# Layer 1's recurrence gates put two to a PSUM bank and one tile later, the state space layer's sums of squares taken later, the attentions' on TensorE

## The reference, cut to what matters

```
# layer 1: gated linear recurrence and mLSTM
u = rmsnorm(x) @ w_in;  x_l, x_m, z = split(u)
r = sigmoid(einsum(conv(x_l), w_a) + b_a)      # 16 blocks of 128x128
i = sigmoid(einsum(conv(x_l), w_x) + b_x)
a = exp(-8 r softplus(-lam))
h = scan(a, sqrt(1 - a^2) * (i * conv(x_l)))   # the recurrence
... mLSTM heads on x_m, each ended by an rmsnorm over its 512 channels
x = x + (concat(h, y_m) * silu(z)) @ w_out
# layer 2: state space layer, 8 groups
y = (ssd_scan(...) + d_skip * xs) * silu(z)
y = rmsnorm per group of 512 channels;  x = x + y @ w_out
# block 3: S5 branch, 4 gated-linear-attention heads, 4 differential-attention heads
o = rmsnorm over 256 channels of each head, then @ w_br
x = x + (g0*y_a + g1*y_b + g2*y_c) @ w_out;  then a gated MLP and a last rmsnorm
```

## Time and profile before

| | us |
|---|---|
| median of 3 runs | 3475.65 (3473.97 to 3477.48) |
| the profiled execution's own time | 3474.76 |
| its span in the trace | 3472.6 |
| PE busy | 3231.7 (93%) |
| DVE busy | 2320.0 (67%) |
| ACT busy | 1833.2 (53%) |
| POOL busy | 687.3 (20%) |

### The profile page before, as it was taken

One profiled execution on the slowest core, in us unless ns is written; L12 is line 12 of the kernel. 1 busy time (PEld: TensorE's weight loads), 2 busy tenths in 40 slices (PEclk: granted clock), 3 DMA queues, 4 the chain that ended last, 5 costly groups with the idle time before them and its releaser, 6 DMA issues.

```text
span 3472.6 us, 54222 instructions
## 1 busy us (share of the span) xinstructions
PE 3231.7 (93%) x21710; PEld 2944.0 (85%) x21710; DVE 2320.0 (67%) x3235; ACT 1833.2 (53%) x2370; POOL 687.3 (20%) x1118
## 2 busy tenths in 40 slices
PE   6999878999999899998998988998999999999998
PEld 6889878888888888887877877888999888888887
DVE  7655767656666776667666766666656788888544
ACT  5544667544665555654555444333444566666443
POOL 2000000010000000012676775776000100000000
PEclk9999988999999999999999999988999999999999
DMA  5435333555444445555433333333555555555554
GB/s 189 141 134 180 126 109 132 191 188 195 163 156 156 151 152 174 173 188 199 158 105 115 129 121 121 132 131 128 199 184 183 188 192 189 189 191 191 188 188 140
DMA packets 158046, 560.54 MB, mean 161 GB/s; under 512 B 17552, under 2 KB 25808, under 8 KB 157152
## 3 DMA queue, kind: packets, MB, share of 16 engines
q1 hardware_dynamic: 157792, 557.06, 47.6%
HBM read 550.64 MB, written 6.36 MB: 160 GB/s over the span
## 4 chain that ended last, share of the span: by engine, by line
PE 68%; DVE 12%; POOL 10%; ACT 6%; issue 3%; DMA 1%; DVEq 0%; ACTq 0%; POOLq 0%; SPq 0%
PE ps L555 68%; POOL TB L1906 5%; DVE WL L1309 3%; POOL PT L1906 2%; ACT WH L890 2%; POOL BX L1906 2%; ACT L880 1%; POOL BS L1906 1%; POOL SQ L1906 1%; DVE XV L1283 1%; DVE XC L1283 1%; DVE BS L1299 0%; DVE X L1283 0%; DMA RAW<-in_w 0%; ACT SQ L880 0%
## 5 line engine op out<-in xcount | busy, mean ns | idle before, releaser
L555 PE MATMUL ps<-XN,WH 128*128 128x256 f32 (+1 forms) x8864 | 1901.3, 308 | 54.2 <-DVE XN L1272 20.0
L890 ACT ACTIVATE WH<-RAW 128x1024 fp32r<-128x1024 f32 x1010 | 1065.1, 1058 | 1309.2 <-PE ps L555 1276.8
L1309 DVE TENSOR_TENSOR WL<-RAW,WH 128x1024 fp32r<-128x1024 f32 x1010 | 1260.9, 1253 | 518.7 <-ACT WH L890 512.4
L555 PEld LDWEIGHTS ps<-XN,WH 128*128 128x128 f32 x8864 | 1468.2, 197 | 144.8 <-issue 22.2
L555 PE MATMUL ps<-XN,WL 128*128 128x256 f32 x5120 | 1461.8, 285 | 0.0
L555 PEld LDWEIGHTS ps<-XN,WL 128*128 128x128 f32 x5120 | 999.8, 195 | 0.0
L555 PE MATMUL ps<-YS,WH 128*128 128x512 f32 (+1 forms) x1088 | 377.7, 392 | 31.6 <-DVE ZB L1272 29.4
L1906 POOL TENSOR_TENSOR RSB<-RSB,SQ 128x256 f32<-128x256 f32 x75 | 87.5, 1166 | 1244.1 <-ACT SQ L880 1243.1
L555 PE MATMUL ps<-YS,WL 128*128 128x256 f32 x1056 | 296.5, 281 | 0.0
L555 PEld LDWEIGHTS ps<-YS,WH 128*128 128x128 f32 x1088 | 203.9, 190 | 81.9 <-DVE ZB L1272 32.3
L1906 POOL TENSOR_TENSOR SQ<-SQ 128x256 f32<-128x256 f32 (+1 forms) x32 | 37.8, 1182 | 1129.5 <-ACT SQ L880 1127.5
(11 more groups left out here) (327 smaller groups left out, 3423.3 us busy)
## 6 DMA issues: line engine op xcount, KB each, us to landing
RAW<-in_w SPq DMA_DIRECT2D x1010, 512.0 KB, 3.3
CSB<-sums SPq DMA_DIRECT2D x64, 128.0 KB, 3.7
scratch<-X SPq DMA_DIRECT2D x2, 2048.0 KB, 7.8
X<-scratch SPq DMA_DIRECT2D x2, 2048.0 KB, 7.7
X<-in_x SPq DMA_DIRECT2D x4, 512.0 KB, 7.9
X<-in_x SPq DMA_DIRECT2D x1, 2048.0 KB, 7.9
out<-X SPq DMA_DIRECT2D x4, 512.0 KB, 2.6
WIF<-in_w_if SPq DMA_DIRECT2D x1, 576.0 KB, 14.3
```

The lines of the kernel that those rows point to most:

```text
L555: return pe.e.matmul(dst, l, r, start=start, stop=stop, skip_group_check=True)
L890: act.e.activation(WH[:, w % NH, :], RAW[:, w % NB, :], ACT.Copy).then_inc(*act.one(("wh", w)))
L1309: dve.e.tensor_tensor(WL[:, w % NB, :], RAW[:, w % NB, :], WH[:, w % NH, :].bitcast(F32), SUB).then_inc(*dve.one(("wl", w)))
```

## The change

Three edits. In layer 1 the gates of pair q are multiplied after the first `xl` tile of pair q+1, not right behind pair q's own `zl` tiles; the two `ra` blocks share one bank (columns 0 to 255 and 256 to 511), the two `ix` blocks another, and ACT reads both halves once the second block is done. The forced ends of `xl` and `zl` in each pair are gone. In layer 2 the chain has 20 steps: POOL adds at step 13, PE multiplies at 15, ACT takes the root at 16, DVE scales at 17, ACT copies at 18, DVE ends at 19; its forced end stands after the second `zs` tile of the next group. In the attentions POOL no longer adds: PE multiplies both halves by ones into one sum.

```
-    "tail": 6, ... "ssd": 16, ...
+    "tail": 6, ... "ssd": 20, ...
...
-    for q in range(8):
-        for i in range(2):
-            p.append(whole(tile("xl", (2 * q + i,), "e_w_in", 128 * (2 * q + i)), 16))
-        for i in range(2):
-            p.append(whole(tile("zl", (2 * q + i,), "e_w_in", 4096 + 128 * (2 * q + i)), 16))
-        p += [End("xl", (2 * q + 1,)), End("zl", (2 * q + 1,))]
+    for q in range(9):
+        if q < 8:
+            p.append(whole(tile("xl", (2 * q,), "e_w_in", 128 * (2 * q)), 16))
         if q:
-            p.append(End("tail", (q - 1,)))
-        for kind, w in (("ra", "e_lru_wa"), ("ix", "e_lru_wx")):
+            for kind, w in (("ra", "e_lru_wa"), ("ix", "e_lru_wx")):
+                for i in range(2 * q - 2, 2 * q):
+                    p.append(whole(tile(kind, (i,), w, (i, 0), "lru"), 1))
+            p.append(Go("tail", (q - 1,)))
+        if q < 8:
+            p.append(whole(tile("xl", (2 * q + 1,), "e_w_in", 128 * (2 * q + 1)), 16))
             for i in range(2):
-                p.append(whole(tile(kind, (2 * q + i,), w, (2 * q + i, 0), "lru"), 1))
-        p.append(Go("tail", (q,)))
+                p.append(whole(tile("zl", (2 * q + i,), "e_w_in", 4096 + 128 * (2 * q + i)), 16))
+            if q:
+                p.append(End("tail", (q - 1,)))
...
-        if g:
-            p.append(End("ssd", (g - 1,)))
-        else:
+        if g == 0:
             p.append(End("dts", ()))
...
             if j == 0:
                 p.append(Go("ssd", (g,)))
+            if j == 1 and g:
+                p.append(End("ssd", (g - 1,)))
...
-                if start:
+                if start and t.x == "lru" and t.args[0] % 2:
+                    open_[id_] = open_[t.kind, t.args[0] - 1]
+                elif start:
...
-                    dst = banks[0][:, 0:256]
+                    c = 256 * (t.args[0] % 2) if t.x == "lru" else 0
+                    dst = banks[0][:, c:c + 256]
...
-                    pe.wait_ge(*at("gsq", h))
-                    mm(b[:, 0:256], ones, SQ[:, 0, 0:256]).then_inc(*pe.one(("gn", h)))
+                    pe.wait_ge(*at("gsqr", h))
+                    mm(b[:, 0:256], ones, SQ[:, 0, 0:256], True, False)
+                    mm(b[:, 0:256], ones, SQ[:, 0, 256:512], False, True).then_inc(*pe.one(("gn", h)))
```

More of the change, by code:

```diff
@@ L740, in ssd @@
                        True).then_inc(*pe.one(("ymm", g, e_)))
-                if s == 11:
+                if s == 12:
                     kept.discard(holder_of("yb", g, 0))
                     kept.discard(holder_of("yb", g, 1))
-                if s == 13:
+                if s == 15:
                     b = take("side", "y2s", g)
@@ L859, in diff @@
                     b = take("side", "dnm", h)
-                    pe.wait_ge(*at("dsq", h))
-                    mm(b[:, 0:256], ones, SQ[:, 0, 0:256]).then_inc(*pe.one(("dnm", h)))
+                    pe.wait_ge(*at("dsqr", h))
+                    mm(b[:, 0:256], ones, SQ[:, 0, 0:256], True, False)
+                    mm(b[:, 0:256], ones, SQ[:, 0, 256:512], False, True).then_inc(*pe.one(("dnm", h)))
             def last():
@@ L995, in ra @@
             def ra(j, s):
[L996 to L999, removed]
-            def ix(j, s):
-                act.wait_ge(*at("tile", "ix", j))
-                fn(IB[:, j % 2, :], bank("ix", j)[:, 0:256], ACT.Sigmoid, ("ixd", j), ("free", "ix", j),
-                   bias=cv("lru_bx", j))
+                if j % 2:
+                    act.wait_ge(*at("tile", "ra", j))
+                    if j > 1:
+                        act.wait_ge(*at("lruscan", j // 2 - 1))
+                    for i in range(2):
+                        fn(RB[:, i, :], bank("ra", j - 1)[:, 256 * i:256 * i + 256], ACT.Sigmoid, ("free", "ra", j - 1),
+                           bias=cv("lru_ba", j - 1 + i))
+            def ix(j, s):
+                if j % 2:
+                    act.wait_ge(*at("tile", "ix", j))
+                    for i in range(2):
+                        fn(IB[:, i, :], bank("ix", j - 1)[:, 256 * i:256 * i + 256], ACT.Sigmoid, ("ixd", j),
+                           ("free", "ix", j - 1), bias=cv("lru_bx", j - 1 + i))
             def tail(p, s):
@@ L1086, in ssd @@
                         fn(SQ[:, w, :], flat(YB[:, 2 * w:2 * w + 2, :]), ACT.Square, ("ysqr", g))
-                if s == 13:
+                if s == 16:
                     act.wait_ge(*at("y2s", g))
                     rsqrt(RS3, bank("y2s", g)[:, 0:256], 512, ("rsy", g), ("free", "y2s", g))
-                if s == 14:
+                if s == 18:
                     act.wait_ge(*at("yn", g))
@@ L1587, in ssd @@
                     tt(YB, YB, ZB, MUL, ("yz", g))
-                if s == 14:
+                if s == 17:
                     dve.wait_ge(*at("rsy", g))
@@ L1591, in ssd @@
                         stt(YB[:, j, :], YB[:, j, :], cv("gnorm", 4 * g + j), RS3, MUL, MUL, ("yn", g))
-                if s == 15:
+                if s == 19:
                     dve.wait_ge(*at("y2h", g))
@@ L1934, in ssd @@
             def ssd(g, s):
-                if s == 12:
+                if s == 13:
                     pool.wait_ge(*at("ysqr", g))
                     halves(("ysq", g))
[L1939 to L1947, removed]
             def phases(b, r):
@@ L1992, in gpsimd @@
                 "wo": lambda n, s: squares(3, n), "dn": lambda n, s: squares(4, n), "heads": heads, "ssd": ssd,
-                "gla": gla, "diff": diff, "s5": s5})
+                "s5": s5})
         def sync(e):
```

## The result

| | median of runs, us | range, us | runs |
|---|---|---|---|
| before, in the same session | 3476.06 | 3473.97 to 3477.48 | 4 |
| changed | 3380.86 | 3378.83 to 3382.80 | 4 |

The ratio is 0.9726 (95%: 0.9713 to 0.9739), a gain of 95.2 us. The forecast was 3357, a gain of 119; the range 3325 to 3403 holds the time. The profiled execution of the changed kernel took 3382.8 us, the slowest of its four runs, and its span is 3380.7.

The account below looks back on a forecast made before the run. PE, busy 93% of the span, was taken as the bound, leaving its idle and low-clock time to gain. Layer 2's 49, layer 1's 43 and the attentions' 27 sum to 119 us, giving 3357 us, range 3325 to 3403.

Parts of the forecast that it names:

- Layer 2, forecast 49 (43 to 52): Layer 2: later chain removes each group's 4.29 us wait and 2.9 us of clock, less one unit at group 7.
- The charge of 2.9 us at group 7: Layer 2, last group: step 19 comes where PE needs the projection's last four blocks, costing one unit, 2.9 us.
- Layer 1, forecast 43 (0 to 69): Layer 1: waits for ZB and RB go; 36 us from seven pairs plus 7 at the first boundary.
- Without them the seven pairs take 218.5: Layer 1 recurrence: DVE's waits IB and WH, 35.7 us, vanish, so 254.2 us becomes 218.5, 31.2 a pair.
- The first rival: Layer 1: ACT's and DVE's mutual waits stretch, giving 0 to 10 us; 3395; chance 0.20, including less from attentions.
- The slower rival: Layer 1: PE waits for WL every unit and stays at 1.2 GHz, losing 131 us; 3531; chance 0.04.
- The attentions, forecast 27 (15 to 35): Attentions: PE no longer waits for POOL's additions; 23.5 us from two large waits, plus head 0's 3.72 and smaller terms.
- 6.8 us in three waits: Whole kernel: remainder of PE's sum-of-squares waits, one being layer 2's eighth group, taken as 1.9 us.
- what is late next is POOL, whose ordinary round is untouched: Attentions, forced ends: POOL's ordinary round keeps its time, so the two large waits count 23.5 us.
- Head 0's 3.72 [...] counts in full: Attentions, head 0: its 3.72 us wait falls where POOL has idle time, so all of it is gained.
- 2.4 us for POOL's additions: Attentions: of POOL's eight dropped additions, 1.18 us each, two lie where POOL is late, gaining 2.4 us.
- The small third rival: Attentions: PE only moves its wait to HH, giving 0 to 10 us instead of 27; 3379; no separate chance given.

Follow-up runs that it names:

- e2: Kernel before with only layer 2's edit, the 20-step chain and its later forced end: 3429.88 us, ratio 0.9870.
- e7: Changed kernel with Tanh for every Silu, Sigmoid, Ln and Exp in layer 1's zl, ra, ix and tail: 3361.08 us, ratio 0.9671 to before.
- e8: Changed kernel with layer 1's mLSTM head steps from 5 on one unit later, PE's sum two: 3383.40 us, ratio 0.9734 to before.
- e9: e3 with POOL still adding the halves of the squares, into a place nobody reads: 3455.61 us, ratio 0.9941 to before.
- e1: Kernel before with only layer 1's edit, new gate order and shared banks: 3438.66 us, ratio 0.9893.
- e6: Kernel before with only layer 1's new gate order, each of the four gate blocks in its own bank: 3468.27 us, ratio 0.9979.
- e5: Kernel before with only layer 1's shared banks, gates in the old order: 3458.58 us, ratio 0.9950.
- e4: e3 with POOL's addition kept for the four linear heads, so only the differential heads are edited: 3458.14 us, ratio 0.9948 to before.
- e3: Kernel before with only the attentions' edit, PE summing both halves in all eight heads: 3456.48 us, ratio 0.9948.
- e10: Changed kernel with six unused matmuls by ones added on PE ahead of a root's sum, before the attentions: 3380.59 us, ratio 0.9726 to before.
- e11: Changed kernel with twelve unused matmuls by ones added on PE ahead of a root's sum, before the attentions: 3381.37 us, ratio 0.9723 to before.
- e12: Changed kernel with layer 1's remainder subtractions of tail and heads moved from DVE to POOL: 3385.73 us, ratio 0.9741 to before.

## Why the prediction was right, and where it was off

**Layer 2, forecast 49 (43 to 52): right.** The stage is 48.9 us shorter. No wait for POOL's squares is left in it, and a group takes 67.8 us at clock 1.00 (forecast 67.7; the earlier trace rows has 74.9 at 0.96). So a wait of 4.29 us did cost 7.1, wait and clock together. e2, which has this edit alone, agrees: 47.3 us of the stage and no wait on POOL's squares left in it. The charge of 2.9 us at group 7 is there too, as one wait of 2.45 us ahead of the projection's last four blocks. PE's timeline of the changed kernel:

```profile
1366.77 0.47 PE L557 MATMUL ps<-YS,WH 128*128 128x512 f32 x1 [2.45 <-DVE YS L1284]
```

**Layer 1, forecast 43 (0 to 69): mechanism right, size 9 too large.** The named waits went, and the clock rose from 0.89 to 0.96 (forecast over 0.95). The step that was mis-sized is "Without them the seven pairs take 218.5": DVE's waits `IB` and `WH`, 35.7 us in the earlier trace rows, were taken to vanish once PE no longer stood still. They fell by half. Two more of DVE's waits from 368 to 623 us before, beside those of the earlier trace rows:

```profile
DVE TH L1272 <- ACT TH L880: 9.3, 5, 2.5
DVE EB L1272 <- ACT EM L880: 9.2, 2, 4.8
```

DVE's waits in the changed kernel's stage:

```profile
DVE WL L1321 <- ACT WH L897: 12.6, 10, 3.1
DVE TH L1284 <- ACT TH L887: 7.4, 4, 2.5
...
DVE IB L1284 <- ACT IB L887: 4.5, 2, 2.2
```

The two fell to 17.1, which is 18.6 less and not 35.7. `TH`, where DVE waits for ACT's logarithms and exponentials, was 9.3 and is still 7.4; the heads' wait for `EM`, 9.2, is 0.9 and made up for a part. What is left of DVE's waits is for ACT, with 0.3 us for PE. The pairs, from one reading of `ra` to the next, take 33.0 us on average (373.56 to 571.33 in six) and not the 30 to 32 that the text gave as the sign of being right. The first rival, that ACT and DVE stretch with the free space, holds in part, and e7 shows how: the table loads between their steps. The sum costed only the one added load, and read the 36 others as given. The heads' part was missed as well; two of PE's waits, of the changed kernel, where before `EB` had 2.1 us in one and POOL's `SQ` none in this stage:

```profile
412.42 1.65 PE L557 MATMUL ps<-EB,CS 128*128 128x256 f32 x4 [5.01 <-DVE EB L1284]
...
557.55 1.23 PE L557 MATMUL ps<-SQ,CS 128*128 128x256 f32 x2 [3.55 <-POOL SQ L1918]
```

e8 shows that such a wait is no cost of its own: moved, it comes back as `WL`. The slower rival did not come: PE meets `WL` five times in the stage, 8.9 us in all, and the clock rose.

**The attentions, forecast 27 (15 to 35): the waits went, the gain is 11.5, under the range of the part.** The small steps first. The sum counted three waits, 26.9 us; in the kernel before there are five in this stage:

```profile
PE ps L555 <- POOL SQ L1906: 31.7, 5, 14.0
```

Two more, of 4.35 and 0.41 us, were left in the "6.8 us in three waits" of which layer 2 has one. All five are gone. PE's sums now wait for ACT alone, little (changed kernel, where the earlier trace rows has 9.22 and 14.00):

```profile
1986.94 1.13 PE L557 MATMUL ps<-SQ,CS 128*128 128x256 f32 x4 [0.69 <-ACT SQ L887]
...
2026.62 1.18 PE L557 MATMUL ps<-SQ,CS 128*128 128x256 f32 x4 [1.83 <-ACT SQ L887]
```

POOL's two long waits, 13.55 and 16.88 in the earlier trace rows, are 3.48 and 4.54 in the changed kernel, under the 6 that the text named:

```profile
2003.35 1.30 POOL L1918 TENSOR_TENSOR BS<-BS,TB 128x512 f32<-128x512 f32 x1 [3.48 <-ACT BS L887]
...
2050.66 1.80 POOL L1918 TENSOR_TENSOR BS<-BS,TB 128x512 f32<-128x512 f32 x1 [4.54 <-ACT BS L887]
```

Idle time of PE fell by 24.0, against the 31.7 of the waits: 2.8 came back as `HH`, 2.5 as waits for ACT's squares, and 2.4 at `DOS`, the scaled output of the differential heads (0.9 to 3.3). Two terms were off. The smaller: POOL's part. From the first of these rows to the second it is 47.31 us, from 2092.23 to 2148.19 it was 55.96. That is 8.65 less, where the sum had 13.6, since what lies between got slower. Before, and then changed:

```profile
2092.23:2131.31 39.08, 25.08 (x179) 23.31 (x179) 20.14 (x30) 17.73 (x27) 29.51 (x63) 0.81 0.27 95
```

```profile
2003.35:2046.12 42.77, 37.64 (x260) 34.59 (x259) 29.71 (x43) 21.54 (x31) 33.35 (x62) 0.92 0.37 124
```

POOL's 62 instructions take 33.35 us, 63 took 29.51, and DVE is now busy 29.7 us beside them, not 20.1: the work that stood still before is now done next to POOL's. The single instructions show it: POOL's `BX` product of 128x256 took 0.72 us twice before, with DVE idle, and 1.24 and 1.60 with DVE at work; now DVE is at work beside all four, and they take 0.72 to 1.60. The step "what is late next is POOL, whose ordinary round is untouched" was wrong in its last half. The 2.4 us for POOL's additions were wrong too: e9 shows 0. Their price of 1.18 us was a mean over two shapes; these eight, of 128x256, took 0.72 to 1.52 us, most of them 0.72. And "Head 0's 3.72 [...] counts in full" holds for that trace and not as a rule: with POOL still adding there, the wait is 2.6 us in e1 and e6, 1.0 in e5 and none in e2 and e4.

The larger: the clock, which the sum left as it was, with a credit for falls saved in the other two parts and none here. At equal clock the edit gives 22 us (747.4 to 725.2), by e3 21. In the changed kernel 10.7 of them go back as a lower clock. Where that begins can be seen at one and the same wait. Before, the row and the 8 us from it on:

```profile
1734.81 0.62 PE L555 MATMUL ps<-HH,CR 128*32 128x256 f32 x2 [2.15 <-DVE HH L1272]
...
1734.81:1742.81 8.00, 8.00 (x54) 6.88 (x55) 5.72 (x8) 5.83 (x9) 6.80 (x16) 1.00 0.26 93
```

Changed:

```profile
1650.71 0.62 PE L557 MATMUL ps<-HH,CR 128*32 128x256 f32 x2 [2.16 <-DVE HH L1284]
...
1650.71:1658.71 8.00, 8.00 (x33) 6.60 (x34) 3.10 (x3) 3.40 (x4) 6.22 (x19) 0.59 0.06 24
```

The wait is 2.15 and 2.16 us long, PE is busy through the 8 us behind it in both, and the clock is 1.00 in the one and 0.59 in the other: 54 matmul records against 33. Up to there PE did the same too: in 8 us that end 0.15 us ahead of the matmul it has 46 records and 6.00 us busy in both, at clock 1.00. The wait is the same, the outcome isn't. All 14 traces have this wait, 56.5 us into the stage and 2.14 to 2.19 us long. The clock of the 8 us behind it is 1.00 in before and e9, 0.79 in e1 to e4, e6, e10, e11 and e12, and 0.58 to 0.60 in changed, e5, e7 and e8. At 2.15 us it was 1.00 and 0.79, at 2.19 us 0.79 and 0.58, so a small difference in length doesn't sort them either. The last stage's +3.6 us is a second such place: behind a wait of 3.00 us at the start of `zs`, in both kernels, PE does 67 records in 8 us before and 46 now.

```profile
2469.03:2477.03 8.00, 8.00 (x67) 8.00 (x68) 4.13 (x6) 2.95 (x5) 0.00 (x0) 1.00 0.88 333
```

```profile
2373.42:2381.42 8.00, 8.00 (x46) 8.00 (x47) 1.93 (x3) 1.46 (x3) 0.00 (x0) 0.64 0.88 316
```

Changed, e10 and e11 have 0.64 here, the other eleven traces 1.00, and the last stage is about 3 us longer in these three than in the rest.

**The sum.** 119 forecast, 92 in the profiled executions, 95 by the medians: layer 1 short by 9, the attentions by 15.5, the last stage by 3.6, layer 2 and the stretch behind layer 1 even or 1 better. The small third rival (attentions give little, 3379) came nearest to the time, but for another reason than it named: PE's wait was not moved to `HH`, whose sum rose by just 2.8. Luck had little part in the sum: nearly all its misses point one way. Only inside the attentions did errors meet: 4.8 us of waits were left out, and 2.4 us for POOL's additions were counted that were worth nothing.

## What to carry to other kernels

Read a ring of banks together with the order of those who take them: here the order alone gave 7 us, the sharing alone 17, both 37, and either half tested by itself would have been put down as small. When a wait is removed in a stage whose helpers are busy 75 to 80%, take the helpers' waits for each other (table loads among them) as the new pace, not their busy times. A gain in a stage full of short waits is known no better than its clock; compare such stages by idle time and by busy time apart, since here the first fell by 24.0 us and the second rose by 12.5, half of that. And a wait that one trace shows in such a stage may be absent in the next without any edit, as head 0's was.

## What the runs showed of the hardware

*The clock behind a short wait isn't a function of the wait.* Waits of 2.15 and 2.16 us were followed by 2.4 GHz in one kernel and mostly 1.2 GHz in the other, with PE busy in the windows shown, and over 14 traces the same wait had three outcomes (clock 1.00, 0.79 and about 0.59 over 8 us). Over the attentions' stage kernels with 57 to 60 us of idle PE lost from 42.5 to 54.0 us. The Trainium skill (TensorE: Matmul & The Clock Gate, HAM oscillation — how this bites in real kernels) says that the way back to the full clock is paid at every such wait, and layer 2 agrees, where a wait of 4.29 us in each group cost 7.1. What decides between the outcomes at 2.15 us was not found: the two kernels made to shift the stage hardly moved it, and that stays open.

*DVE and POOL hold each other up, one whole instruction at a time.* With POOL's subtractions in the stage, the 128x1024 product on DVE took 1346 ns on average against 1241, and POOL's own took 1800 ns for 128x512 and 2423 for 128x1024. The Trainium skill (SBUF — State Buffer, Who interferes with whom) says that a DVE instruction with two inputs in SBUF contends with a GpSimd instruction that reads there, and that the one that comes second is held for the whole of the first. The traces agree: in e12 a product that began first took its 1.21 to 1.22 us, and each of the eight that began second ended 1.08 to 1.09 us after POOL's instruction, nearly its own length.
